# Encoder kernel on one core: the second closing pass of five token tiles on ScalarE and GpSimd instead of VectorE

## The reference

```
x = layer_norm(ALPHA * x + mix, ln1_g, ln1_b)
x = layer_norm(ALPHA * x + conv_ffn(x, w_up, conv_w, conv_b, w_down), ln2_g, ln2_b)

def layer_norm(x, g, b):
    mu = mean(x); var = mean(square(x - mu))          # over the 1024 channels of a token
    return (x - mu) * rsqrt(var + EPS) * g + b
```

## Time and profile before

| | |
|---|---|
| time, median of three runs | 963.26 us |
| profiled execution | 963.37 us |
| its span | 961.6 us |
| TensorE busy | 944.0 us, 98% |
| VectorE busy | 786.2 us, 82% |
| ScalarE busy | 471.7 us, 49% |
| GpSimd busy | 282.2 us, 29% |

### The profile page before, as it was taken

How to read it: one execution, slowest core, us unless ns; L and a number is a source line. 1 busy time by engine, 2 the same in 40 slices (tenths; PEclk the granted TensorE clock), 3 DMA queues, 4 the chain that set the end, 5 groups by cost and what they waited for, 6 DMA issues and landing times.

```text
span 961.6 us, 12084 instructions
## 1 busy us (share of the span) xinstructions
PE 944.0 (98%) x4402; PEld 773.6 (80%) x4402; DVE 786.2 (82%) x1147; ACT 471.7 (49%) x706; POOL 282.2 (29%) x257
## 2 busy tenths in 40 slices
PE   7999999999999999999999999999999999999996
PEld 6888887667888788888888888888888888888885
DVE  5666488987886899889798888898888699977798
ACT  5575467868014664554455445445545754333200
POOL 2300327993940000010010001100000199990032
PEclk9999999999999999999999999999999999999999
DMA  8245153928031136365555464654527886564212
GB/s 312 83 87 175 22 132 136 304 45 305 10 144 43 67 91 160 79 164 132 121 142 134 100 172 100 142 148 105 153 66 262 339 340 232 190 229 171 96 66 109
DMA packets 110811, 142.06 MB, mean 148 GB/s; under 512 B 21164, under 2 KB 72320, under 8 KB 110753
## 3 DMA queue, kind: packets, MB, share of 16 engines
q1 hardware_dynamic: 104352, 129.69, 40.6%
q0 software_dynamic: 5184, 9.44, 7.2%
q10 hardware_dynamic: 1216, 2.17, 0.7%
HBM read 112.18 MB, written 47.97 MB: 167 GB/s over the span
## 4 chain that ended last, share of the span: by engine, by line
PE 93%; DVE 4%; issue 2%; DMA 1%; ACT 0%; POOL 0%; SPq 0%; DVEq 0%
PE ps L792 28%; PE ps L794 28%; PE ps L793 28%; PE ps L1042 2%; PE ps L1021 2%; DVE bn L1301 1%; DVE acc L1862 1%; PE ps L998 1%; PE ps L1154 1%; PE ps L999 1%; DMA acc<-in_x_prompt 1%; PE ps L827 1%; DVE pT L1518 0%; DVE prob L1510 0%; DVE mv L1305 0%
## 5 line engine op out<-in xcount | busy, mean ns | idle before, releaser
L792 PE MATMUL ps<-db_hi,ga_hi 128*128 128x512 f32 x252 | 98.0, 389 | 0.0
L793 PE MATMUL ps<-db_lo,ga_hi 128*128 128x512 f32 x252 | 98.0, 389 | 0.0
L794 PE MATMUL ps<-db_hi,ga_lo 128*128 128x512 f32 x252 | 98.0, 389 | 0.0
L792 PE MATMUL ps<-x1h,wa_hi 128*128 128x512 f32 x192 | 75.6, 394 | 0.0
L794 PE MATMUL ps<-x1h,w_lo 128*128 128x512 f32 x192 | 74.8, 389 | 0.0
L2220 ACT ACTIVATE hc<-U,taps 128x512 f32<-128x512 f32 x60 | 48.7, 813 | 53.1 <-DVE U L1697 41.5
L793 PE MATMUL ps<-x1l,wa_hi 128*128 128x512 f32 x192 | 74.7, 389 | 0.0
L737 POOL TENSOR_TENSOR acc<-acc,gain_bc 128x1024 f32<-128x1024 f32 x12 | 40.5, 3374 | 84.6 <-ACT bias_bc L1912 84.6
L2225 ACT ACTIVATE hc<-hc 128x512 f32<-128x512 f32 x44 | 27.9, 633 | 71.3 <-DVE hc L1714 71.3
L1912 ACT ACTIVATE ga_hi<-ga_raw 128x1536 fp32r<-128x1536 f32 x21 | 31.3, 1490 | 62.0 <-DMA db_raw<-in_w_down 28.8
L1298 DVE TENSOR_TENSOR ga_lo<-ga_raw,ga_hi 128x1536 fp32r<-128x1536 f32 x21 | 48.5, 2310 | 9.9 <-ACT ga_hi L1912 9.9
(11 more groups left out here) (314 smaller groups left out, 2892.5 us busy)
## 6 DMA issues: line engine op xcount, KB each, us to landing
w_raw<-in_w_up SPq DMA_DIRECT2D x44, 512.0 KB, 4.9
ga_raw<-gs_scratch SPq DMA_DIRECT2D x21, 768.0 KB, 4.6
ts_scratch<-in_w_down SPq DMA_DIRECT2D x12, 768.0 KB, 14.9
gs_scratch<-gsum SPq DMA_DIRECT2D x9, 1024.0 KB, 4.5
db_raw<-ts_scratch SPq DMA_DIRECT2D x12, 768.0 KB, 6.2
db_raw<-in_w_down SPq DMA_DIRECT2D x9, 768.0 KB, 6.5
ts_scratch<-in_w_down POOLq DMA_DIRECT2D x18, 256.0 KB, 5.1
gs_scratch<-gated SPq DMA_DIRECT2D x9, 512.0 KB
```

Of the source, the lines that this page charges most:

```text
L792: pe.matmul(out, whi, xhi, start=start, stop=False, skip_group_check=onto)
L793: pe.matmul(out, whi, xlo, start=False, stop=False, skip_group_check=onto)
L794: return pe.matmul(out, wlo, xhi, start=False, stop=stop, skip_group_check=onto)
```

## The change

Tiles 0 to 4 (`SHARED`) get their second closing pass in two parts. ScalarE multiplies the tile by rstd (`scale_tile`), once VectorE's first pass of the tile and the tile's rstd are there. GpSimd adds the bias (`shift_tile`); in its queue the sum of tile t stands behind `last_rstd` of tile t+1. VectorE has no `finish_bias` for these tiles. SyncE waits for `y_shifted` before it sends them. Tiles 5, 6 and 7 are closed as before.

```diff
+SHARED = (0, 1, 2, 3, 4)
+def shared_before(t):
+    return sum(1 for s in SHARED if s < t)
...
             for t in range(TT - 1):
-                sp.wait_ge(y_ready, t + 1)
+                if t in SHARED:
+                    sp.wait_ge(y_shifted, SHARED.index(t) + 1)
+                else:
+                    sp.wait_ge(y_ready, t + 1 - shared_before(t))
                 sp.dma_start(y_tiles[t], acc[:, t, :]).then_inc(y_out, 16)
             for half in range(2):
                 cols = slice(half * 512, (half + 1) * 512)
-                sp.wait_ge(y_ready, TT + half)
+                sp.wait_ge(y_ready, TT + half - len(SHARED))
...
+            def shift_tile(t):
+                pool.wait_ge(y_scaled, SHARED.index(t) + 1)
+                pool.tensor_tensor(acc[:, t, :], acc[:, t, :], bias_bc[:], ALU.add).then_inc(y_shifted, 1)
+
             for t in range(TT):
                 last_rstd(t)
+                if t - 1 in SHARED:
+                    shift_tile(t - 1)
...
             def finish_gain(t):
                 for cols in pieces(t):
                     chain.mark(dve.scalar_tensor_tensor(...))
+                gained[t] = chain.k
...
-                    if t and half == 0:
+                    if t and half == 0 and t - 1 not in SHARED:
                         finish_bias(t - 1)
...
+            def scale_tile(t):
+                act.wait_ge(dve_chain, gained[t])
+                act.wait_ge(rstd_ready, 2 * TT + t + 1)
+                act.activation(acc[:, t, :], acc[:, t, :], ACT.Copy, scale=rstd[:, t:t + 1]).then_inc(y_scaled, 1)
+
+            for t in SHARED:
+                scale_tile(t)
```

More of the change, by code:

```diff
@@ L398, in build @@
             "p1_out", "u2_out", "u3_out", "c11_sum", "c12_sum", "c22_sum", "hc_ready", "conv_done", "gelu_done", "g_ready")]
-        dn_hi, dn_lo, dn_ps, dn_act, dn_dve, y_ready = [sem(n) for n in (
-            "dn_hi", "dn_lo", "dn_ps", "dn_act", "dn_dve", "y_ready")]
+        dn_hi, dn_lo, dn_ps, dn_act, dn_dve, y_ready, y_scaled, y_shifted = [sem(n) for n in (
+            "dn_hi", "dn_lo", "dn_ps", "dn_act", "dn_dve", "y_ready", "y_scaled", "y_shifted")]
+        gained = {}
         block = ctx.enter_context(nc.Block())
```

## The result

The changed kernel takes 963.9 us against 962.56 of the kernel before, medians of 22 runs each; the ratio is 1.0012, with a 95% interval of 1.0007 to 1.0018. The prediction said 1.19 us more, 964.5 in all, and no difference by that bound. Its 964.5 stood on the median of three runs, 963.26, which is 0.7 above the 962.56 of 22.

What follows compares the result with a forecast made beforehand. TensorE's matmuls bound the kernel until about 915 us, then VectorE, 0.75 us late by the last half. The profiled 963.37 plus 1.19 gave 964.56, against the median 964.45; taken as 964.5, range 962.5 to 966.0.

Steps and rivals of the forecast that it cites:

- Base: Whole kernel: matmuls set the time until about 915 us, 2.72 us a half in the closing; VectorE does after.
- Removed passes: VectorE's closing: five second passes of 1.20 us leave, plus 0.13 of waiting each; worth at most 0.75 us.
- rival A: Closing: no harm from GpSimd's tile 4 sum; last sum at 953.93, -0.53 us, 962.8 in all; chance 0.07.
- ScalarE at no cost: Five 128x1024 scalings on ScalarE, 1.04 to 1.24 us by similar rows, cost nothing, even at 3 us.
- Stores at no cost: The five early stores wait for GpSimd, the last until 949.04, landing some 10 us before the end; cost nothing.
- Shifts 0 to 3 at no cost: GpSimd's bias sums of tiles 0 to 3 take 2.40 us each, 0.94 us to spare per tile; cost nothing.
- What reads PSUM is not shut out: VectorE's PSUM sums run untouched, in 1.27 us a pair, beside a GpSimd pass; only two-SBUF-tensor instructions shut GpSimd out.
- Shift 4 against bias pass 5: GpSimd's tile 4 sum starts 0.55 us before VectorE's tile 5 bias pass, which stands until 948.91; +1.19 us.
- B: Closing: VectorE's tile 5 bias pass gets in before GpSimd's tile 4 sum; +0.06 us, 963.4; chance 0.05.
- C: Closing: VectorE and GpSimd share memory at half speed, tile 5 bias pass takes 2.4; +0.7 us, 964.1; chance 0.06.
- D: Closing: GpSimd becomes the bound, its sums take 3.79 us; +3.9, 967.2; chance 0.10 including sums well above 2.9 us.

Runs made afterwards that it cites:

- e1: Changed kernel without GpSimd's five bias sums (tiles 0 to 4 go out without bias); ratio 0.9992 to the kernel before, stretch from first to last sum 40.96 us.
- e6: Changed kernel with each of GpSimd's five bias sums run twice; ratio 1.0061 to the kernel before, stretch from first to last sum 47.43 us.
- e2: Changed kernel with VectorE's bias pass of tile 5 reading its second tensor from PSUM instead of SBUF; ratio 0.9994 to the kernel before.
- e5: Changed kernel with GpSimd's bias sum of tile 4 whole, but waiting until VectorE's bias pass of tile 5 is done; ratio 0.9999 to the kernel before.
- e7: Changed kernel with GpSimd's bias sum of tile 4 cut into two halves directly behind each other, no added wait; ratio 1.0000 to the kernel before.
- e3: Changed kernel with only tiles 0 to 3 shared out instead of 0 to 4; ratio 1.0010 to the kernel before.
- e4: Changed kernel with GpSimd's bias sum of tile 4 in halves, waiting for VectorE's bias passes of tiles 5 and 6; ratio 0.9996 to the kernel before.

## Why the prediction was right

- Base. TensorE sets the time until the closing and goes at 2.72 us a half in it; confirmed (the sums of the second halves of tiles 0 to 5 in the changed kernel are 5.44 apart). What comes ahead of it was as before but for an offset of 1.6 us that was there by 142 us.
- Removed passes. Forecast -0.53 with shifts that harm nobody (rival A's 953.93); e1 measured -0.52. The 0.60 us from statistics to a next instruction that waits for nothing, for which no row stood, is 0.62 in e6 (931.10 to 931.72).
- ScalarE at no cost: confirmed, 1.16 us a scaling, idle for over 4 us between two of them.
- Stores at no cost: confirmed, the tail is 7.08 against 7.14.
- Shifts 0 to 3 at no cost, 2.40 each by the lower end of the row and not 3.79 by its median: confirmed, 2.393 to 2.413. The choice rested on what stands beside the rows, and e6 shows longer ones at once (3.30) where gain passes come between.
- What reads PSUM is not shut out: confirmed, shifts 0 to 3 and e2. The forecast named VectorE's two sums at 784.55 as running beside a GpSimd pass; that pass is this row of the kernel before, which takes about 2.4 us of work from 784.5 on:

```profile
783.09 3.81 POOL L739 TENSOR_TENSOR acc<-acc,bias_bc 128x1024 f32<-128x1024 f32 x1
```

- Shift 4 against bias pass 5. Forecast: start 0.08 behind the power, a hold of 1.72 (947.19 to 948.91), +1.19 in all. Measured: the shift starts 0.03 ahead of the power's recorded end (944.89 against 944.92), 0.11 earlier than forecast; the release is 0.20 ahead of the shift's end, where two earlier instructions had given 0.13 (767.35 and 767.48); the hold is 1.52, +0.99 in all. The mechanism was right and its size 0.2 too large. For the start I took the gap from two steps of which the second waits for the first's result, where the shift waits for nothing of GpSimd's own. That the times give +1.2, so near the forecast's 1.19, is luck: their interval, 0.7 to 1.7, can't tell 1.19 from 0.99.
- The range. 962.5 to 966.0 and "no difference" would have held under A, B and C as well. That the forecast had the right cause is shown by the rows of bias pass 5 and shift 4, and not by the time.
- The rivals. A fell by the 2.80. B did not come by itself; e5 makes its order with an added wait and costs 0.22 against the kernel before where I had 0.06, since shift 4 starts 1.43 us behind the start of bias pass 5 (946.99 to 948.42) and not 1.20. C, sharing at half speed, fell by 2.80 against 2.4, by shift 4, which took 2.39 where sharing would have made it longer too, and by e5 and e7, where the hold is what is left of one whole instruction. D did not come, and its arithmetic for 3.79 us shifts was not tested: e6 tested the load, in pairs of shorter instructions. One step of that arithmetic fails there: it let the slips of gain passes 2 to 5 add up, although VectorE has some 1.2 us idle in each tile, and in e6 these passes keep 5.44 under holds of 1.1 to 1.2.
- The rule of the Trainium skill that was weighed ("SBUF — State Buffer", section "SBUF: two separate sides"), that whoever starts first has the pair of ports for its whole instruction and the other fully blocks, agrees with the traces for two SBUF inputs: the holds of 1.52 in the changed kernel, 0.74 in e5 and 0.42 in e7 are each what was left of one GpSimd instruction. By recorded times the pass that stood begins its own 1.28 us of work 0.20 us ahead of the shift's end. Whether GpSimd lets go that early, or its end is recorded late, these traces can't tell.

## What to carry to other kernels

Before a pass moves from VectorE to GpSimd, list what VectorE still runs beside it with two SBUF tensors, and look at which semaphore releases both: here the last shift and the first bias pass left wait for the same power, and they met in the changed kernel and in e3. One meeting costs the rest of the instruction that came first, so place the GpSimd pass where VectorE reads PSUM or takes statistics, or cut it to fit that gap; shorter instructions also let the other engine in between. And ask first what the move can win: here VectorE was only 0.75 us late, so 0.75 was the most, and the five passes gave 0.52 where nothing met them (e1).

## What the runs showed of the hardware

- VectorE's bias pass of 128x1024 takes 1.28 us with its second tensor in PSUM, as with both in SBUF, and so it runs beside a GpSimd pass at no loss to either (e2).
- The hold goes by single instructions: a VectorE pass gets in between two GpSimd instructions that follow each other directly, where the second waits for nothing (e7: it stands 0.42 us, the two take 3.52) or for the first (e6: gain pass 3 in 1.29, the second instruction in 3.30).
- GpSimd starts a pass 0.03 us ahead of the recorded end of an independent instruction before it (changed kernel: 944.92, 944.89), 0.08 behind one whose result it waits for (944.28 to 944.36), and 0.15 behind the end of a VectorE pass that releases it (e4: 946.82 to 946.97; e5: 948.27 to 948.42).
